# S5's GELU and gate moved two block steps back in layer 0 and nine in layer 1 of a hybrid decoder step

## What is computed

```python
y5, s_re_new, s_im_new = _s5_scan(su, ...)          # B,T,256
y5 = jax.nn.gelu(y5)
y5 = y5 * jax.nn.sigmoid(y5 @ s5_glu_w + s5_glu_b)
mixed = jnp.concatenate([o_hg, o_rt, y5], axis=-1) @ w_out
```

## The kernel before, in words

| piece | engine | step |
|---|---|---|
| `s5_out_sample` | TensorE | 15, 7 |
| `s5_gelu_argument` | VectorE | 16, 8 |
| GELU's sigmoid | ScalarE | 17, 9 |
| first product | VectorE | 17, 9 |
| `glu` 0 and 1 | TensorE | 18, 10 |
| gate sigmoids | ScalarE | 19, 11 |
| second product | VectorE | 19, 11 |

## Time and profile before

### The profile page before, as it was taken

One profiled execution on the slowest core, in us unless ns is written; L12 is line 12 of the kernel. 1 busy time (PEld: TensorE's weight loads), 2 busy tenths in 40 slices (PEclk: granted clock), 3 DMA queues, 4 the chain that ended last, 5 costly groups with the idle time before them and its releaser, 6 DMA issues. The chain is left out here.

```text
span 874.6 us, 18226 instructions
## 1 busy us (share of the span) xinstructions
PE 767.2 (88%) x7662; PEld 723.4 (83%) x7662; DVE 553.0 (63%) x974; ACT 387.7 (44%) x672; POOL 36.2 (4%) x44
## 2 busy tenths in 40 slices
PE   3768778989799778999997889799897999999994
PEld 3768767778699778999986888697796999999993
DVE  7995995345666799655445788734556665466543
ACT  5644133343565422565346525243435553355423
POOL 4000010200000000000010002011000000000000
PEclk9998879889989999999996999787997999999998
DMA  8432112334235344554542332313151555555531
GB/s 335 144 121 75 51 50 73 128 150 121 73 126 183 126 138 147 197 170 140 174 145 69 97 102 88 125 49 105 49 169 51 177 183 194 174 182 175 191 99 50
DMA packets 30577, 113.59 MB, mean 130 GB/s; under 512 B 3520, under 2 KB 3728, under 8 KB 29984
## 3 DMA queue, kind: packets, MB, share of 16 engines
q1 hardware_dynamic: 27936, 101.83, 35.4%
q0 software_dynamic: 1984, 9.52, 2.9%
q10 hardware_dynamic: 576, 1.08, 0.3%
HBM read 108.24 MB, written 4.18 MB: 129 GB/s over the span
## 5 line engine op out<-in xcount | busy, mean ns | idle before, releaser
L1288 DVE TENSOR_TENSOR w_low<-w_raw,w_high 128x1024 fp32r<-128x1024 f32 x192 | 239.3, 1247 | 206.5 <-ACT w_high L944 204.2
L899 PE MATMUL stream<-a_high,w_high 128*128 128x264 f32 x1024 | 316.8, 309 | 42.5 <-DVE a_low L1293 31.1
L944 ACT ACTIVATE w_high<-w_raw 128x1024 fp32r<-128x1024 f32 x192 | 202.1, 1054 | 278.5 <-PE stream L901 250.3
L900 PE MATMUL stream<-a_low,w_high 128*128 128x264 f32 x1024 | 305.4, 298 | 2.5 <-issue 2.5
L901 PE MATMUL stream<-a_high,w_low 128*128 128x264 f32 x1024 | 304.5, 297 | 0.0
L899 PEld LDWEIGHTS stream<-a_high,w_high 128*128 128x128 f32 x1024 | 207.4, 203 | 56.0 <-issue 28.6
L900 PEld LDWEIGHTS stream<-a_low,w_high 128*128 128x128 f32 x1024 | 208.4, 204 | 3.1 <-issue 2.7
L901 PEld LDWEIGHTS stream<-a_high,w_low 128*128 128x128 f32 x1024 | 207.3, 202 | 0.0
L899 PE MATMUL stream<-h_high,w_high 128*128 128x264 f32 x512 | 149.3, 292 | 11.3 <-DVE w_low L1288 9.6
L900 PE MATMUL stream<-h_low,w_high 128*128 128x264 f32 x512 | 145.2, 284 | 0.0
L901 PE MATMUL stream<-h_high,w_low 128*128 128x264 f32 x512 | 144.9, 283 | 0.0
(11 more groups left out here) (328 smaller groups left out, 747.2 us busy)
## 6 DMA issues: line engine op xcount, KB each, us to landing
w_raw<-in_weights SPq DMA_DIRECT2D x192, 512.0 KB, 3.3
mats<-in_matrices POOLq DMA_DIRECT2D x2, 1024.0 KB, 5.1
S_hg<-in_state_hg POOLq DMA_DIRECT2D x2, 768.0 KB, 5.8
out_hg_s<-S_hg POOLq DMA_DIRECT2D x2, 768.0 KB, 3.8
consts<-in_constants POOLq DMA_DIRECT2D x1, 1484.5 KB, 9.1
X<-in_xT ACTq DMA_DIRECT2D x4, 264.0 KB, 5.7
out_y<-X SPq DMA_DIRECT2D x1, 1056.0 KB, 4.0
S_rt<-in_state_rt POOLq DMA_DIRECT2D x2, 512.0 KB, 6.8
```

Source lines behind the costliest of these rows:

```text
L899: pe.matmul(bnk[:, 0:T], wh, xh, start=(first and kk == 0), stop=False)
L900: pe.matmul(bnk[:, 0:T], wh, xl, start=False, stop=False)
L944: act.activation(w_high[:, n % SPLIT_SLOTS, :], w_raw[:, n % RAW_SLOTS, :], ACT.Copy).then_inc(high_ready, 1)
L1288: put(tt(w_low[:, n % SPLIT_SLOTS, :], w_raw[:, n % RAW_SLOTS, :], w_high[:, n % SPLIT_SLOTS, :].bitcast(F32), ALU.subtract), low_ready)
```

## The change

The constant `GELU_AT` = (18, 17) names the step of `s5_gelu_argument`, and all the others follow from it: the sample output's unit at the step before, the GELU's sigmoid and the first product one step after, the `glu` units two after, the gate sigmoids and the second product three after. In layer 0 each moves from its step to two later, in layer 1 to nine later. Nothing is added or removed. The code places inside a step stay: VectorE's argument stands ahead of `hgrn_sample_add`, `ret_k_decay` and `ret_scores` of its step.

```diff
@@ -95,6 +95,7 @@
 LATER = (2, 0)
+GELU_AT = (18, 17)
 TABLES_AT = UP_B + 11
@@ -113,10 +114,10 @@
-    _plan((15, 7)[_l], ("s5_out_sample",), layers=(_l,))
+    _plan(GELU_AT[_l] - 1, ("s5_out_sample",), layers=(_l,))
     for _f in range(3):
         _plan(13 + _s + _f, ("hg_kv", _f), layers=(_l,))
-    _plan((18, 10)[_l], ("glu", 0), ("glu", 1), layers=(_l,))
+    _plan(GELU_AT[_l] + 2, ("glu", 0), ("glu", 1), layers=(_l,))
@@ -1070,10 +1071,10 @@ (ScalarE, mixer_work)
-                if c == (17, 9)[l]:
+                if c == GELU_AT[l] + 1:
                     act.wait_ge(gelarg_ready, l + 1)
                     act.activation(gel, gel, ACT.Sigmoid, scale=GELU_C1).then_inc(gel_ready, 1)
-                if c == (19, 11)[l]:
+                if c == GELU_AT[l] + 3:
                     for m in range(2):
                         b, fu = got(l, ("glu", m))
@@ -1623,7 +1624,7 @@ (VectorE, mixer_work)
-                if c == (16, 8)[l]:
+                if c == GELU_AT[l]:
                     s5_gelu_argument(l)
```

## The result

| | before | after |
|---|---|---|
| median of the runs (20 and 20) | 879.05 us (869.12 to 885.89) | 884.34 us (875.87 to 893.96) |
| ratio | | 1.0115, 95% interval 1.009 to 1.014 |
| span of the profiled execution | 874.6 us | 890.0 us |

The ratio is taken of the fast runs alone, those within 1.5% of the fastest of their kernel, which leaves out seven of the 20 before and two of the 20 after. By it the change costs 1.15% (0.0115 x 879.05 = 10.1 us), where +6.7 us was forecast: 1.5 times the forecast. The size is less firm than the interval suggests. Over all 40 runs the medians are 5.3 us apart and the means 6.8 us, with a 95% interval from 3.8 to 9.8 us, so that the forecast size is not excluded by them; that the change costs time is shown either way.

The account below looks back on a forecast made before the run. TensorE, busy 88% of the span, was taken as the bound. Layer 0's +4.1 us and layer 1's +2.6 us summed to +6.7: 880.4 us at the median, own range 877.5 to 883.5, wide range 872.5 to 888.

Parts of the forecast that it names:

- Layer 0, the score pair: Step 17: `ret_score` 2 and 3 wait for banks VectorE frees in and behind the moved argument; +3.0 us, bounds 0 and 3.5.
- Layer 0, the removed vector work: Steps 16 and 17: taking VectorE's argument and product away gains 0, since `w_low` waits for ScalarE; bound 4.2 us.
- The rival of the vector chain in both layers: VectorE was the late engine at `w_low` of chunks 19 and 14, new homes free: 8.6 us gained, 865.1 us; chance 0.08.
- Layer 0, -0.6 us at step 18: ScalarE's queue ahead of its copies loses two gate sigmoids and gains the GELU's own: 0.6 us gained, bounds 0 and 1.7.
- The gates' new homes: Gate matmuls in full TensorE stretches, layer 0 step 20 and layer 1 step 19: +1.7 us each, bounds 0 and 3.4.
- The even case: Both waits grow by only 1 us and the gates hide in one home: +1.0 us, 874.7 us; chance 0.15.
- Layer 1, the decay: Steps 16 and 17: the argument delays `ret_k_decay`, which frees banks for `tr_hkd`; +3.0 us, bounds 2.3 and 3.5.
- The scores' own wait ends before that: Layer 1, step 16: `ret_score` 1's wait for the sample output's bank ends before `tr_hkd`'s wait and costs nothing more.
- Layer 1, the gain of 2.1 us at the head: Steps 8 to 11: TensorE loses sample and gate matmuls and VectorE can follow; 2.1 us gained, bounds 0.7 and 4.4.
- The clock: Chunks behind both lengthened waits already ran slow and lose nothing more; by the rows, no cost in the sum.
- The rival of the falling clock: Longer waits slow two more chunks and the gates once: 5.3 us on top, 885.7 us; chance 0.17.
- some 4 us higher: What the sum would be by the Trainium skill's rule that idleness puts TensorE to half rate, with two longer waits.

Follow-up runs that it names:

- fill: Changed kernel plus sixteen filler matmuls ahead of `ret_score` 2 in layer 0 and sixteen ahead of `tr_rk` 0 in layer 1; 887.56 us, ratio 1.0123 to before.
- order: Changed kernel with the sample output's unit last in its step and VectorE's argument behind `ret_scores`; 879.39 us, ratio 1.0062 to the kernel before.
- l0_only: Kernel before with only layer 0's pieces moved, two steps later, layer 1 untouched; 876.45 us, ratio 1.0004 to the kernel before.
- glu_wait: Kernel before with only layer 1's gate matmuls moved to the head of step 16, sigmoids and second product following; 878.32 us, ratio 1.0039 to before.

## Why the prediction came out as it did

- **Layer 0, the score pair: right.** +3.0 us was forecast. The wait grew from 1.54 to 4.03 us, and the stretch costs 2.9 us at full clock (fill). order, which takes the bank and the argument away from the pair, brings 1.54 us back.
- **Layer 0, the removed vector work: right.** It gained nothing: `w_low` of chunk 19 now waits 2.5 to 4.1 us for `w_high`, and chunk 16 to 17 takes 9.04 us for 9.05, with 3.4 us of half clock on both sides (two executions each). The rival of the vector chain in both layers falls with it.
- **Layer 0, -0.6 us at step 18: the size holds where the clock allows a reading.** 10.48 to 9.82 us in order, both with 3.4 us of half clock.
- **The gates' new homes: right.** +1.7 us each was forecast, 1.8 us was measured in layer 1 at full clock (6.33 and 6.34 for 4.56 us, in six kernels), 1.87 us from start to start in layer 0. The even case, in which they hide in one of the homes and the waits grow by 1 us only, is refuted: both waits grew by 2.5 to 3 us.
- **Layer 1, the decay: right, by a narrow margin.** 11.48 to 14.35 us in the mean of three, +2.9 for +3.0. "The scores' own wait ends before that" holds by the 0.28 us that `tr_hkd` still waits; nearly all of the waiting, 4.98 us, stands ahead of the scores.
- **Layer 1, the gain of 2.1 us at the head: mis-sized.** It measured 1.4 us (chunks 7 to 12, 30.18 to 28.76 us, with 1.1 us more at half clock). The sample matmuls gave 0.5 us (3.50 to 3.00 us from chunk 7 to 8) and the gates 1.7 us between chunks 10 and 11. Two things took part of it back. TensorE, now earlier, waits 1.67 for 1.30 us for VectorE ahead of chunk 12. That VectorE is full there from `w_low` of chunk 14 on stood in the prediction; that TensorE already waited for it did not. And the gap in `hg_level` 0 that nothing in the profile releases, which the prediction allowed a microsecond either way, grew from 2.73, 2.73 and 3.00 us to 3.05, 3.33 and 3.33:

```profile
514.31 0.22 PE L657 MATMUL mix<-Qg,Kg 64*32 64x16 f32 x3 [2.73 <-issue]
...
532.63 0.49 PE L595 MATMUL mix<-consts,MIX 128*8 128x128 f32 x3 [1.30 <-DVEq L1267]
```

  and after:

```profile
526.20 0.23 PE L659 MATMUL mix<-Qg,scratch 64*32 64x16 f32 x1 [3.05 <-issue]
```

- **The clock: the step that failed.** It read "the chunks behind both waits were slow already and lose nothing more", and the sum put the clock at nothing. In layer 1 it holds: chunks 17 to 20 lost 1.5 us, the gates' share. In layer 0 it doesn't: chunks 17 to 19 ran 6.3 us more at half clock and lost 4.2 us, for 2.4 forecast, and chunks 19 to 24 gave that back (-0.8 us for +1.7, with 5.7 us less at half clock). And I counted the clock only beside the waits that I changed. It fell in other places too: chunks 24 to 26 of layer 1 lost 2.9 us, of which chunks 20 to 24 gave back 2.1, and chunks 24 to 96 of layer 0 lost 1.4. Over all executions the change has 131 us of half clock for 119. The rival of the falling clock asked for 5.3 us on top, two slow chunks behind the waits and slow gates; about 3.4 us on top is what the fit gives, and its place was in the main wrong: order has short waits and as much half clock. The Trainium skill (TensorE: Matmul & The Clock Gate, The HAM clock gate) says that idleness lowers the clock and sustained work raises it. In its direction fill agrees, at the one wait that it filled in part (chunk 18 at 0.99, for 0.74, 0.79 and 0.81 in the changed kernel). As a price for the whole program the rule did not serve. The prediction's own "some 4 us higher" under it, for which it shows no working, was nearer to the 10.1 us of the ratio than its sum, through another place than I had put it.

The sum by terms, with the measured sizes: +2.9 - 0.6 + 1.8 + 2.9 + 1.8 - 1.4 = +7.4 us, 0.7 us above the forecast, all of it from the head of layer 1. It lies inside the interval of the means (3.8 to 9.8 us). The rest to the ratio's 10.1 us, 2.7 us, I put down to half clock in stretches whose TensorE instructions the change doesn't touch (+2.4 us in the table); that is argued, not shown. The fit draws the line elsewhere, 5.5 us for the schedule and 3.4 us for the clock; some of the terms hold half clock of their own, and how the loss divides is not settled closer than that. That the half clock between chunks 24 and 26 comes with a change of layer 1's schedule is what the profiles say throughout (ten against four). How the placing of the matmuls brings it about is open. So is why l0_only, whose trace has the +4 us, shows nothing in its median: the constant of the fit, +2.8 +- 1.8 us, would leave room for both.

## What to carry to other kernels

When a unit moves in a plan that hands out banks in turn, go through the new turn of the banks and ask which engine frees each, and behind what: here the move cost two waits of 2.9 us which no edited instruction made by itself, and swapping two places in the plan (order) took both away. Vector work taken out of a crowded stretch is worth nothing when the next instruction waits for another engine, and matmuls moved into a full stretch cost their whole length; the free home is in a wait of TensorE's own (glu_wait, 0.0 us in that stretch, though the whole kernel did not get faster). Allow the clock a few tenths of a per cent in stretches far behind the edit, and repeat the profile before a stretch with half clock in it is blamed on the change.

## What the runs showed of the hardware that was not expected

- The same program, in separate executions, goes to half clock in different stretches: chunks 24 to 26 of layer 0 took 12.03, 14.01 and 14.45 us in before, with 0, 5.9 and 6.8 us at half clock. Its times spread from 869 to 886 us in 20 runs; how much of that is the clock's is not separated.
- A microsecond at half clock goes with 0.27 us more over the whole program, by the fit. Where TensorE is busy it costs more: chunks 20 to 24 of layer 1 took 26.17 us with none (l0_only) and 29.03 us with 6.8 us of it (fill), 0.42 us for each. Where TensorE waits for VectorE it costs nothing: chunk 16 to 17 of layer 1 took 11.46 to 11.49 us in the eight profiles without the longer wait and without layer 1's sample matmuls there, with 3.0 to 6.2 us at half clock.
- A gap of TensorE between two small matmuls of `hg_level` 0, released by nothing in the profile, depends on what was moved out of the steps around it: 2.72 to 3.00 us in the seven profiles with layer 1's argument and sample matmuls in their old place, 3.05 to 3.38 us in the seven without. Its cause is open.
